# The last residual of a two-layer backbone turned to token rows during routing

## What is computed

```python
for layer in range(DEPTH):
    ...
    h_lat = h_lat + mod_l[2] * (jnp.concatenate([o[1] for o in outs], axis=-1) @ w_out[layer])
    ...
    f_lat = (_rmsnorm(h_lat, g_ffn[layer]) * (1 + mod_l[4]) + mod_l[3]).reshape(-1, d_model)
    ...
        y_lat = _hier_moe(f_lat, *moe_p)
    h_lat = h_lat + mod_l[5] * y_lat.reshape(bsz, n_lat, d_model)
return h_lat
```

## Time and profile before

| | |
|---|---|
| median of three runs | 1990.04 us (1987.12 to 1991.53) |
| profiled execution | 1987.32 us, span 1985.3 us |
| busy in the span | PE 1844.7 us (93%), PE weight loads 1173.5 us, DVE 797.8 us (40%), ACT 566.8 us (29%), POOL 67.3 us |
| chain that ended last | PE 81%, DVE 10%, ACT 3%, DMA 3%, issue 2% |
| mean granted clock of TensorE | 0.972 of full speed |
| DMA | 361.41 MB, 182 GB/s over the span |

### The profile page before, as it was taken

One profiled execution on the slowest core, in us unless ns is written; L12 is line 12 of the kernel. 1 busy time (PEld: TensorE's weight loads), 2 busy tenths in 40 slices (PEclk: granted clock), 3 DMA queues, 4 the chain that ended last, 5 costly groups with the idle time before them and its releaser, 6 DMA issues.

```text
span 1985.3 us, 36978 instructions
## 1 busy us (share of the span) xinstructions
PE 1844.7 (93%) x15991; PEld 1173.5 (59%) x15991; DVE 797.8 (40%) x1710; ACT 566.8 (29%) x1219; POOL 67.3 (3%) x68
## 2 busy tenths in 40 slices
PE   5999999899889989999998999999899897999975
PEld 3554668667654655555554765467667684555533
DVE  3424466678821451011111541356778525111113
ACT  3113233557620321111110523232657422000000
POOL 0000000000010000000000100000000100000001
PEclk9999999989989989999999999999999999999988
DMA  9611110192150777778988512001000306999996
GB/s 379 234 56 43 33 32 22 37 300 68 53 224 22 297 302 290 268 297 302 386 346 342 175 36 98 6 27 54 10 13 1 139 34 251 331 395 396 363 398 223
DMA packets 153025, 361.41 MB, mean 182 GB/s; under 512 B 11704, under 2 KB 73664, under 8 KB 152608
## 3 DMA queue, kind: packets, MB, share of 16 engines
q1 hardware_dynamic: 130128, 316.30, 43.0%
q0 software_dynamic: 6736, 23.99, 3.7%
q10 hardware_dynamic: 16000, 18.75, 2.7%
HBM read 318.26 MB, written 40.77 MB: 181 GB/s over the span
## 4 chain that ended last, share of the span: by engine, by line
PE 81%; DVE 10%; ACT 3%; DMA 3%; issue 2%; SPq 1%; POOL 0%; ACTq 0%; POOLq 0%; DVEq 0%
PE ps L1385 16%; PE ps L974 15%; PE ps L1408 9%; PE ps L1256 7%; PE ps L959 6%; PE ps L1084 4%; PE ps L1118 3%; PE ps L1150 2%; PE ps L919 2%; PE ps L1142 2%; PE ps L1453 2%; PE ps L1366 1%; DMA arena<-in_w_mod 1%; DVE att_small L2172 1%; PE ps L1395 1%
## 5 line engine op out<-in xcount | busy, mean ns | idle before, releaser
L1385 PE MATMUL ps<-arena 128*32 128x256 f32 x6080 | 349.7, 383 | 2.0 <-ACT arena L1869 2.0
L974 PE MATMUL ps<-arena 128*128 128x256 f32 (+2 forms) x1056 | 348.8, 486 | 0.9 <-ACT arena L1650 0.9
L1385 PEld LDWEIGHTS ps<-arena 128*32 128x32 f32 x6080 | 200.4, 111 | 133.3 <-issue 3.7
L974 PEld LDWEIGHTS ps<-arena 128*128 128x128 f32 x1056 | 198.8, 191 | 130.4 <-issue 116.2
L2581 DVE TENSOR_TENSOR arena<-ps,arena 128x128 f32<-128x128 f32 x95 | 27.7, 292 | 413.7 <-ACT arena L1876 413.7
L1408 PE MATMUL ps<-arena 128*32 128x256 f32 x3040 | 183.1, 382 | 0.0
L1256 PE MATMUL ps<-arena 128*128 128x256 f32 (+1 forms) x512 | 143.4, 434 | 2.0 <-DVE arena L2270 2.0
L1084 PE MATMUL ps<-arena 32*128 32x256 f32 (+5 forms) x528 | 130.1, 510 | 3.1 <-ACT arena L1724 2.3
L1876 ACT ACTIVATE arena<-ps 128x128 f32<-128x128 f32 x95 | 26.4, 278 | 370.3 <-PE ps L1385 370.3
L1775 ACT ACTIVATE arena<-ps,att_small 128x768 f32<-128x768 f32 (+2 forms) x160 | 123.3, 773 | 23.8 <-DVE att_small L2172 22.7
L1408 PEld LDWEIGHTS ps<-arena 128*32 128x32 f32 x3040 | 89.3, 109 | 61.2 <-issue 1.0
(11 more groups left out here) (375 smaller groups left out, 2092.2 us busy)
## 6 DMA issues: line engine op xcount, KB each, us to landing
arena<-in_moe_w_gu SPq DMA_DIRECT2D x32, 4096.0 KB, 19.9
arena<-in_moe_w_down SPq DMA_DIRECT2D x32, 2048.0 KB, 12.4
arena<-in_w_mod SPq DMA_DIRECT2D x24, 2048.0 KB, 18.1
y_rows<-zeros_t SPq DMA_DIRECT2D x2, 9216.0 KB, 52.4
arena<-in_w_in SPq DMA_DIRECT2D x6, 2048.0 KB, 8.1
arena<-in_w_in SPq DMA_DIRECT2D x8, 1024.0 KB, 5.7
y_rows<-arena ACTq DMA_DIRECT2D x76, 96.0 KB, 8.0
arena<-in_w_out SPq DMA_DIRECT2D x4, 1536.0 KB, 8.2
```

The costliest lines, as they stand in the source:

```text
L974: last = pe.matmul(PS[:, 4 + k % 2, 0:ch[2]], aT[:, c, t * P:(t + 1) * P], wbuf[:, j % 2, c, 0:ch[2]], start=(c == 0), stop=(c == DC - 1))
L1385: last = pe.matmul(PS[32 * q:32 * q + 32, 2 + g % 2, 0:2 * P], xT(item_par(L, k))[:, a:a + SUB], gate_up_cols(ring_e(L, r), c, q), start=( ...
```

## The change

The residual of layer 1 is final once the output projection is done. The change turns its four latent tiles to token rows during layer 1's routing: eight transposes a tile on PE into banks 0 to 3, and a copy by ACT back into the place in `hT` that the tile was read from (`residual(t)`). Tiles 2 and 3 go before the gates, tiles 4 and 5 behind them. The gates' products now wait for the copies of the first two, and the last two tiles wait for `gates_ready`. The three fill products before the gates are gone, those before the slots' product are two instead of three, and six stand behind it instead of three. The first item's transposes wait for all residual copies. At the end PE does nothing any more, and DVE takes the residual from `hT`.

```diff
+        def residual(t):
+            return hT[:, :, t * P:(t + 1) * P]
...
+                def residual_rows(i, t):
+                    pe.wait_ge(S("ftok_a"), OT0[L] + T)
+                    for c in range(DC):
+                        last = pe.transpose(PS[:, 2 * (i % 2) + c // 4, (c % 4) * P:(c % 4 + 1) * P], residual(t)[:, c], ident)
+                    last.then_inc(S("ftok_ps"), 1)
+
                 if L == LAYERS - 1:
-                    fill_clock(3)
-                    pe.wait_ge(S("ftok_a"), OT0[L] + T)
+                    for i, t in enumerate(tl[:2]):
+                        residual_rows(i, t)
+                    pe.wait_ge(S("ftok_a"), OT0[L] + T + 2)
                     for c in range(DC):
                         g = mod4[:, L, 40 + c, 0:1]
...
-                fill_clock(3 if L else 7)
+                if L == LAYERS - 1:
+                    pe.wait_ge(S("gates_ready"), 1)
+                    for i, t in enumerate(tl[2:], 2):
+                        residual_rows(i, t)
+                fill_clock(2 if L else 7)
                 pe.wait_ge(S("oh_ready"), L + 1)
...
-                fill_clock(3 if L else 6)
+                fill_clock(6)
...
                 if L == LAYERS - 1:
-                    pe.wait_ge(S("gates_ready"), 1)
+                    pe.wait_ge(S("ftok_a"), OT0[L] + 2 * OTN[L])
...
-            for i, t in enumerate(out_tiles(1)):
-                if i == 1:
-                    pe.wait_ge(S("h_done"), G0[1] + NS[1])
-                if i == 2:
-                    pe.wait_ge(S("hT_ev"), G0[1] + NS[1])
-                    pe.wait_ge(S("y_a"), G0[1] + NS[1])
-                for c in range(DC):
-                    last = pe.transpose(PS[:, 2 * i + c // 4, (c % 4) * P:(c % 4 + 1) * P], hT[:, c, t * P:(t + 1) * P], ident)
-                last.then_inc(S("tok_ps"), 1)
...
+                def residual_rows(i, t):
+                    act.wait_ge(S("ftok_ps"), OT0[L] + OTN[L] + i + 1 + i // 2)
+                    act.activation(residual(t), PS[:, 2 * (i % 2):2 * (i % 2) + 2, :].rearrange("p b (c n) -> p (b c) n", n=P),
+                                   ACT.Copy).then_inc(S("ftok_a"), 1)
+
                 if L == LAYERS - 1:
-                    act.wait_ge(S("ftok_ps"), OT0[L] + OTN[L] + 1)
+                    for i, t in enumerate(out_tiles(L)[:2]):
+                        residual_rows(i, t)
+                    act.wait_ge(S("ftok_ps"), OT0[L] + OTN[L] + 3)
                     act.activation(gate_row, PS[:, 0:2, :].rearrange("p b n -> p (b n)"), ACT.Copy)
                     act.activation(gate_sub, PS[:, 2, 0:2 * P], ACT.Copy).then_inc(S("gates_ready"), 1)
+                    for i, t in enumerate(out_tiles(L)[2:], 2):
+                        residual_rows(i, t)
...
-                dve.wait_ge(S("tok_ps"), NT + i + 1)
+                dve.wait_ge(S("ftok_a"), OT0[1] + OTN[1] + i + 1)
                 dve.wait_ge(S(f"g_in{i}"), 32 * ((NT + 3 - i) // 4 + 1))
                 o = restok[:, i, :]
-                link(dve.scalar_tensor_tensor(out=o, in0=y_pair(i, 1), scalar=wtok[:, NT + t:NT + t + 1],
-                                              in1=PS[:, 2 * i:2 * i + 2, :].rearrange("p b n -> p (b n)"), op0=mul, op1=ALU.add))
+                link(dve.scalar_tensor_tensor(out=o.rearrange("p (c n) -> p c n", n=P), in0=y_pair(i, 1).rearrange("p (c n) -> p c n", n=P),
+                                              scalar=wtok[:, NT + t:NT + t + 1], in1=residual(t), op0=mul, op1=ALU.add))
```

## The result

Twenty runs of each kernel on the same chips: the changed kernel takes 1996.68 us in the median (1987.18 to 2008.26), the kernel before 1991.83 us (1983.17 to 1996.52). The medians are 4.9 us apart. The measured ratio, which is not that of the two medians, is 1.0038 with a 95% interval of 1.0022 to 1.0054: 7.6 us slower, with 4.4 to 10.8 us as bounds. It is larger than the distance of the medians, as nine of the changed kernel's twenty times lie at 2000 us or more; the means are 7.1 us apart. The forecast was +5.9 us.

The account below looks back on a forecast made before the run. The prediction took the chain through layer 1's routing, with the slots' product at 1676.34 us, and the final store and gathers as the bound; 6.9 + 1.8 + 0.2 - 3.0 = +5.9 us on 1990.04 gave 1995.9 us, range 1991.0 to 2002.5.

Parts of the forecast that it names:

- The end is worth 0: End of the program: removing the 32 transposes and reading the residual from SBUF gives 0 us.
- Four steps queue ahead of the slots' product: Layer 1's routing: four PE steps in a row, each waiting for ScalarE, start the slots' product 6.9 us later.
- the rival without a fall of the clock: Layer 1's routing: all steps at full clock, slots' product +5.5 us, total +2.7 us, 1992.7 us; chance 0.17 with smaller mixtures.
- transposes at the low clock: Before the gates: sixteen residual transposes of two tiles on PE take 3.40 us at the low clock.
- copies: Routing: PE waits for ScalarE's copy of the second tile, 1.2 us, and of the gates, 1.45 us.
- The clock falls in the wait that the removed fills left: Before the first new transposes: PE idle 4.6 us, after which the clock falls to its low level.
- I take half: Gates in layer 1's routing: low clock throughout would cost 3.6 us, none 0; half taken, +1.8 us.
- Six fills give 3.0 us back: Behind the slots' product: six fills keep the clock high, so the first item's 128 records end 3.0 us sooner.
- stuck low clock: Rival: clock low until behind the slots, product 13.7 us late, total +12.1 us, 2002.1 us; chance 0.2.
- the rule on transposes: Trainium skill's statement that transposes don't count as busy time for PE's clock and full speed doesn't engage for them.
- The run's own time: Whole program: the profiled execution of 1987.32 us would take 1993.2 us with the change.
- the slots' product starting at 1682 to 1685 us: Sign of a right forecast in layer 1's routing: the slots' product starts then instead of at 1676.34 us.

Follow-up runs that it names:

- e3: Kernel before without the 32 transposes at the end, VectorE adding hT as it lies; profiled only: 19.9 us ranks to slots, 17.1 us slots to 128 records.
- e2: Changed kernel with five fill products in PE's wait ahead of the first residual transposes; ratio 1.0011 to the kernel before.
- e4: Changed kernel with three fills behind the slots' product instead of six; profiled only: 29.0 us ranks to slots, 15.6 us slots to 128 records.
- e6: Changed kernel with the residual's 32 transposes issued as products with the identity; profiled only: 28.1 us ranks to slots, 15.6 us slots to 128 records.
- e8: Changed kernel with the gates' eight 128-column products first, then the eight of 32 columns; profiled: 18.5 us ranks to slots, 15.6 us slots to 128 records.
- e11: Same kernel as e8, timed and profiled again; ratio 0.9994 to the kernel before, 20.3 us ranks to slots.
- e12: Changed kernel unchanged, profiled a second time: 21.9 us ranks to slots, 15.6 us slots to 128 records.
- e1: Kernel before with six fill products behind the slots' product instead of three; ratio 0.9985.
- e7: Kernel before with four fills ahead of layer 1's last logits, five ahead of the gates and six behind the slots; ratio 0.9986.
- e10: Kernel before with the gates' products grouped by width, six fills ahead of the slots' product and six behind; ratio 0.9977.

## Why the prediction was right

The time (+4.9 us by the medians and +7.6 by the ratio, against +5.9), the direction and the mechanism came out: work queued ahead of the slots' product on PE, with a fall of the clock in the wait in front of it. One term was mis-sized, the gates at the low clock. That the number is so near is luck in part: by their pieces the two courses seen cost 3.6 and 9.9 us, and the forecast lies between them without having either. Point by point:

- **The end is worth 0**: right, by e3 and by the equal distances in the changed kernel.
- **Four steps queue ahead of the slots' product**: right. With the clock up all the way (e2) the delay is 5.1 us, where the rival without a fall of the clock had 5.5. The single terms: transposes at the low clock 3.3 to 3.7 us (3.40), copies 1.11 and 1.39 (1.2 and 1.45), two fills 1.7 (1.8). The working has 1.2 us for the copies in the forecast and 1.3 in the rival without a fall, which changes nothing.
- **The clock falls in the wait that the removed fills left**: right, in all six profiles in which nothing fills it (changed, e4, e6, e8, e11 and e12).
- **"I take half" of the gates at the low clock, +1.8 us**: this is the term that was mis-sized. In the changed kernel's order no profile has the half: the gates ran wholly at the low clock, 10.4 us, or wholly at the full one, 6.1 us. (In the order of before the clock fell within them in e1, e3 and e7.) The factor is 1.7 and not the 1.6 taken from the slots' rows, so the term is +4.4 or 0. In the first case the second transposes are slow too, 1.5 us, which I had only in the rival. So the product is 6.9 + 4.4 + 1.5 = 12.8 us late by the corrected sum (12.9 measured), or 6.9 (6.7 in e12), and never the 8.7 forecast. The premise behind the half, that a low stretch lasts 3.42 or 6.83 us, was wrong as well: here one lasted 23.9 us.
- **Six fills give 3.0 us back**: the size is right against the profile shown (15.63 against 18.69), but e3 and e4 put the loss of three fills at 1.4 and 0 us in other executions. The wait of 2.1 to 2.4 us doesn't always lower the clock.
- **The rival "stuck low clock"** (0.2) was nearly what the first profile shows: it had the product 13.7 us late, and it was 12.9. It was too rare in my chances: two of three profiles took that course. Its ground in the rule on transposes fell, though. That the gates keep the clock low, because they alternate between two widths of weights, is argued and not shown: it stayed low for all of them in changed and e4, and came back within them in e11, where they stand by kind.
- **The run's own time**: the profile came out at 1992.42 us where I had 1993.2 for it, but by cancelling: 10.3 us lost from ranks on, 5.0 us of luck ahead of them. The same luck is in the sign "the slots' product starting at 1682 to 1685 us": it started at 1684.24, but counted from the ranks that is 12.9 us late, which on the time scale of the profile before is 1689.3 and near the stuck clock's 1690.0.

Whether the median's +4.9 us is a mixture of about +3.6 us (e12 against the profile before: 21.9 + 15.6 against 15.3 + 18.7) and +9.9 us (28.2 + 15.6 against the same) can't be settled, since only a few executions were profiled; the kernel before also varies (34.0 and 37.0 us for the two pieces).

## What to carry to other kernels

Work that fits into an engine's idle time must also stand behind what is waited for in that engine's queue: with 32 transposes and the waits for their copies ahead of the slots' product it came 5 us late at full clock, and with half of them moved into the wait behind it 0.6 us. Before taking filler work out of a wait, look at what comes after the wait: here a fall of the clock lasted through all of the gates in two of three profiles. And judge an edit of a few microseconds by pieces between marks of the profile, in several executions, since whole times differed by 5 us before the first edited instruction in the first pair of profiles, and by up to 18 us over all of them.

## What the hardware showed that was not expected

- Products whose weights alternate between 128 and 32 columns cost 0.75 us a pair at full clock and 1.29 us at the low one (1667.40 to 1668.69); the same sixteen products grouped by width take 2.65 us in all, 0.33 us a pair (e8). Neither kernel has them grouped. In the changed order the grouping takes 3.4 us off the way to the slots' product (21.9 in e12, 18.5 in e8); in the order of before VectorE ends that piece at full clock, and it stays at 15.1 us (e10) against 15.3.
- A PE that is busy 9.12 of 10.24 us, with those alternating gates, stayed at 1.2 GHz throughout (changed kernel, 1668.70 to 1678.94), and in e7 the clock fell while they ran, 2.1 us after their start and after a wait of 1.47 us. Behind stretches in which PE did nothing but transposes it came back, in the changed kernel (at 1682.35) and in e8 (at 1667.50).
- The same first set of transposes stands behind the same wait in the changed kernel, e12 and e8. In the first the clock was still low behind it, in the other two it came back while they ran (1666.1 and 1667.5), and the courses of the changed kernel and of e12, one and the same program, are 6.3 us apart at the slots' product. What decides between them these runs leave open.
